# A two-block transformer on one core: differential attention moved beside its own input projection, and single read-outs at the ends of stages

## What is computed

```python
def diff_attention(h, w_in, lq1, lk1, lq2, lk2, subln_w, w_out, rel_table, lambda_init):
    qkv = h @ w_in
    q, k, v = jnp.split(qkv, 3, axis=-1)
    q = q.reshape(B, S, DA_HEADS, 2, DA_HEAD_DIM)
    k = k.reshape(B, S, DA_HEADS, 2, DA_HEAD_DIM)
    v = v.reshape(B, S, DA_HEADS, DA_V_DIM)
...
        logits = jnp.einsum('bqhmd,bkhmd->bmhqk', qb, kb).astype(jnp.float32) * scale + bias
        logits = jnp.where(dist >= 0, logits, -jnp.inf)
        p = jax.nn.softmax(logits, axis=-1)
        attn = p[:, 0] - lam * p[:, 1]
        outs.append(jnp.einsum('bhqk,bkhd->bqhd', attn.astype(vb.dtype), vb))
...
    o = rmsnorm(o, subln_w) * (1.0 - lambda_init)
    return o.reshape(B, S, DA_HEADS * DA_V_DIM) @ w_out
```

## Time and profile before

| | us |
|---|---|
| median of 3 runs | 1363.32 (1362.34 to 1363.82) |
| the profiled execution, its own time | 1364.6 |
| its span | 1362.9 |
| PE busy in the span | 1303.9 (96%) |
| DVE busy | 926.0 (68%) |
| ACT busy | 730.5 (54%) |

### The profile page before, as it was taken

How to read it: one execution, slowest core, us unless ns; L and a number is a source line. 1 busy time by engine, 2 the same in 40 slices (tenths; PEclk the granted TensorE clock), 3 DMA queues, 4 the chain that set the end, 5 groups by cost and what they waited for, 6 DMA issues and landing times.

```text
span 1362.9 us, 24156 instructions
## 1 busy us (share of the span) xinstructions
PE 1303.9 (96%) x8322; PEld 1153.5 (85%) x8322; DVE 926.0 (68%) x1573; ACT 730.5 (54%) x1300; POOL 265.6 (19%) x274
## 2 busy tenths in 40 slices
PE   7998999999999999999999979999999987999997
PEld 5986668999999988888889957888889975888885
DVE  6766755655555798776556688886657766877564
ACT  5456644666444455664444475665445755566441
POOL 3001101222010113441010002442104610344010
PEclk9996557999999999999999989999999998999997
DMA  7331021565554655655565503665464531665540
GB/s 233 112 119 54 0 63 47 178 182 182 184 185 155 214 173 169 185 186 190 191 205 174 173 28 96 204 193 186 161 209 126 186 124 31 185 185 185 186 154 31
DMA packets 204435, 205.28 MB, mean 151 GB/s; under 512 B 6079, under 2 KB 203829, under 8 KB 204361
## 3 DMA queue, kind: packets, MB, share of 16 engines
q1 hardware_dynamic: 202101, 202.73, 47.2%
q10 hardware_dynamic: 2260, 1.58, 0.4%
HBM read 203.22 MB, written 1.06 MB: 150 GB/s over the span
## 4 chain that ended last, share of the span: by engine, by line
PE 81%; DVE 11%; ACT 4%; issue 1%; POOL 1%; DMA 0%; DVEq 0%; SPq 0%; POOLq 0%; ACTq 0%
PE PS L1437 27%; PE PS L1438 14%; PE PS L1432 9%; PE PS L1431 9%; PE PS L1433 9%; DVE wlo L859 3%; PE PS L1613 3%; PE PS L1592 3%; DVE x L836 2%; DVE tmp L872 1%; PE PS L1635 1%; PE PS L1601 1%; ACT whi L444 1%; DVE h L882 1%; PE PS L1549 1%
## 5 line engine op out<-in xcount | busy, mean ns | idle before, releaser
L859 DVE TENSOR_TENSOR wlo<-raw,whi 128x1024 fp32r<-128x1024 f32 (+1 forms) x388 | 469.1, 1211 | 210.2 <-ACT whi L444 208.4
L444 ACT ACTIVATE whi<-raw 128x1024 fp32r<-128x1024 f32 (+1 forms) x388 | 404.1, 1045 | 361.6 <-PE PS L1438 212.1
L1437 PE MATMUL PS<-x,whi 128*128 128x512 f32 x832 | 293.8, 397 | 4.9 <-DVE x L836 4.5
L1431 PE MATMUL PS<-x,whi 128*128 128x256 f32 (+2 forms) x928 | 265.7, 286 | 7.6 <-DVE wlo L859 4.2
L1437 PE MATMUL PS<-hid,whi 128*128 128x512 f32 x768 | 267.0, 394 | 0.0
L1432 PE MATMUL PS<-x,whi 128*128 128x256 f32 (+2 forms) x928 | 265.3, 286 | 0.0
L1433 PE MATMUL PS<-x,wlo 128*128 128x256 f32 (+2 forms) x928 | 263.8, 284 | 0.0
L1438 PE MATMUL PS<-x,wlo 128*128 128x256 f32 x832 | 235.1, 283 | 0.0
L1438 PE MATMUL PS<-hid,wlo 128*128 128x256 f32 x768 | 212.7, 277 | 0.0
L1437 PEld LDWEIGHTS PS<-x,whi 128*128 128x128 f32 x832 | 157.1, 189 | 42.9 <-DVE x L836 6.8
L1343 POOL TENSOR_TENSOR acc<-acc,sq 128x256 f32<-128x256 f32 (+2 forms) x72 | 64.9, 901 | 652.7 <-ACT sq L472 651.9
(11 more groups left out here) (274 smaller groups left out, 1710.3 us busy)
## 6 DMA issues: line engine op xcount, KB each, us to landing
raw<-in_mlp_w SPq DMA_DIRECT2D x64, 1024.0 KB, 5.7
raw<-in_w_mlp_up SPq DMA_DIRECT2D x32, 1024.0 KB, 5.5
raw<-in_w_mlp_down SPq DMA_DIRECT2D x32, 1024.0 KB, 5.2
raw<-in_w_in_conv SPq DMA_DIRECT2D x12, 1024.0 KB, 5.1
raw<-in_attn_w_in SPq DMA_DIRECT2D x12, 1024.0 KB, 5.2
raw<-in_mlstm_w_in SPq DMA_DIRECT2D x12, 1024.0 KB, 5.3
raw<-in_w_in_attn SPq DMA_DIRECT2D x9, 1024.0 KB, 8.0
raw<-in_w_out_attn SPq DMA_DIRECT2D x4, 1024.0 KB, 8.5
```

What stands on the lines that cost most here:

```text
L444: A(part_view(whi, b), raw_view(b), ACT.Copy).then_inc(w_hi, 1)
L859: V.tensor_tensor(part_view(wlo, b), raw_view(b), f32(part_view(whi, b)), ALU.subtract).then_inc(w_lo, 1)
L1431: mm(dst, whi_b, xs_hi, start=first, stop=False)
L1437: mm(dst.rearrange("p (a t) -> p a t", a=2), std_cols(whi[b % RING], k), xs_both, start=first, stop=False)
```

## The change

**Attention beside d_in.** The blocks of d_in come in the order q, k, v of one pair of heads (two blocks each), then the next pair. One loop over 62 **slots** drives PE, ACT and DVE. In slots 0 to 47 PE does half a block of d_in (4 of 8 k); in slots 48 to 53 it does k 0 to 2 and then 3 to 5 of the first three blocks of d_out, in slot 57 their k = 6, and after the last slot their k = 7 and the blocks 3 to 7. The four tiles of pair p have slots 12p+10, 13, 16, 19; the last pair's have 46, 48, 50, 52. For a tile in slot s: scores and max in s, exp in s+1, probabilities in s+2, transposes and their copy in s+4, the product with V in s+5; a head's norm and y follow 5 to 8 slots behind its second tile. The values are transposed head by head into the small bank MISC. Banks: 3 for d_in's results instead of 4, one for each map, one for transposes, one for the head's output.

**Scores.** Plain fp32, one matmul for each map over 128 or 256 columns, straight from `dz`; `dzh` and `dzl` and their splitting are gone.

**Single read-out.** The last block of c_in, c_out, d_out and m_out and the block o = 3 of each half of dn1, dn2 and dn3 run as products, and DVE reads them without `halves`.

The diff, cut to its core:

```diff
-    dz = sb("dz", [P, KB * S], F32, s)
-    dzh, dzl = sb("dzh", [P, 2 * KB * S], F32R, s), sb("dzl", [P, 2 * KB * S], F32R, s)
+    dz = sb("dz", [P, 3 * KB * S], F32, s)
...
+    if stage == "d_in":
+        return D_IN_BANK[o % 3]
     return (O[stage] + o) % PSR
...
-MAP_BANK = ((0, 1), (2, 5))
+MAP_BANK = (5, 6)
 A_SPLIT_AT = tuple(NT * HEADS + 3 * n for n in range(RING))
-D_FLIP_AT = (4, 7)
-D_T_BANK = 3
+D_FLIP_AT = (5, 8)
+D_TILE_AT = {12 * p + 10 + (2 if p == 3 else 3) * r: 4 * p + r for p in range(4) for r in range(4)}
+D_VALUE_AT = {12 * p + 11 + 2 * e: 2 * p + e for p in range(4) for e in range(2)}
+D_SLOTS = 62
+D_T_BANK, D_O_BANK, D_IN_BANK = 2, 7, (3, 0, 1)
...
-            residual(n, j, tok, (psum_read, O[stage] + j + 1) if n == 1 else (Z["out_h"], KB * (n // 2 - 1) + j + 1))
+            residual(n, j, tok, (psum_read, O[stage] + j + 1) if n == 1 or j == KB - 1 else (Z["out_h"], (KB - 1) * (n // 2 - 1) + j + 1))
...
-            act.wait_ge(Z["cs_ready"], f + 1)
+            if f < KB - 1:
+                act.wait_ge(Z["cs_ready"], f + 1)
+            else:
+                act.wait_ge(psum_read, O["c_in"] + j + 1)
             A(at(yh, f, LAST), cs[:, f % 2, :], ACT.Copy).then_inc(Z["y_hi"], 1)
...
+    for s in range(D_SLOTS):
+        n = d_tile(s - 1)
+        if n is not None:
             d_exp(n)
...
+        hd = D_VALUE_AT.get(s)
+        if hd is not None:
+            act.wait_ge(Z["d_vt"], hd + 1)
+            A(dvt[:, :, hd * P:(hd + 1) * P], PS[:, MISC, 0:S].rearrange("p (a c) -> p a c", a=TS), ACT.Copy)\
+                .then_inc(Z["d_vtok"], 1)
+        n = d_tile(s - 4)
+        if n is not None:
+            d_prob_t(n)
...
-            A(d_sq[:, hd % 2, :], PS[:, O_BANK[hd % 2], 0:S], ACT.Square).then_inc(Z["d_osq"], 1)
-        hd = head_at(n, 6)
...
+        hd = d_head(s - 7)
...
+        if s < 6 * KB and s % 2:
+            split_hi(B["d_in"] + s // 2 + RING)
...
-            if n == 1:
+            if n == 1 or j == KB - 1:
                 V.tensor_tensor(at(h, j, tok), PS[:, bank(stage, j), 0:tok[1]], at(h, j, tok), ALU.add).then_inc(psum_read, 1)
             else:
                 halves(tmp[:, j % 2, 0:S], bank(stage, j)).then_inc(psum_read, 1)
...
-                    if m:
...
                     else:
                         mul(t, PS[:, bank(dn, o), 0:tok[1]], rstd2[:, 0:tok[1]]).then_inc(psum_read, 1)
...
+            if f < KB - 1:
+                halves(tmp[:, f % 2, 0:S], bk).then_inc(psum_read, 1)
+                dve.wait_ge(psum_read, O["c_in"] + j + 1)
+                mul(cs[:, f % 2, :], tmp[:, f % 2, 0:S], cy[:, f, :]).then_inc(Z["cs_ready"], 1)
+            else:
+                mul(cs[:, f % 2, :], PS[:, bk, 0:S], cy[:, f, :]).then_inc(psum_read, 1)
...
     norm(4, LAST)
-    dve.wait_ge(w_used, B["d_in"])
-    for j in range(3 * KB):
-        dve.wait_ge(w_used, B["d_in"] + j + 1)
-        dst = d_z(j) if j < 2 * KB else zb(dz, j - 2 * KB)
-        if 4 <= j < 2 * KB:
-            dve.wait_ge(Z["d_lo"], j - 3)
-        mul(dst, PS[:, bank("d_in", j), 0:S], rstd[:, 0:S]).then_inc(psum_read, 1)
-        split_lo(B["d_in"] + j + RING)
-        if 2 <= j < 2 * KB + 2:
-            dve.wait_ge(Z["d_hi"], j - 1)
-            V.tensor_tensor(zb(dzl, j - 2), d_z(j - 2), f32(zb(dzh, j - 2)), ALU.subtract).then_inc(Z["d_lo"], 1)
...
+    for s in range(D_SLOTS):
+        if s < 6 * KB and s % 2:
+            j = s // 2
+            dve.wait_ge(w_used, B["d_in"] + j + 1)
+            mul(d_z(j), PS[:, bank("d_in", j), 0:S], rstd[:, 0:S]).then_inc(psum_read, 1)
+        n = d_tile(s)
+        if n is not None:
+            if n == 0:
+                dve.wait_ge(Z["d_bias"], 2)
             d_max(n)
-        if n >= 7 and (n - 7) % TS == 0 and (n - 7) // TS < HEADS:
...
+        n = d_tile(s - 2)
+        if n is not None:
+            d_prob(n)
+        hd = d_head(s - 7)
...
-        if 2 <= n < N_D + 2:
-            d_prob(n - 2)
-        if n >= 9 and (n - 9) % TS == 0 and (n - 9) // TS < HEADS:
...
+        hd = d_head(s - 8)
+        if hd is not None:
...
+        if s < 6 * KB and s % 2:
+            split_lo(B["d_in"] + s // 2 + RING)
     out_proj("d_out", 5, LAST)
...
-        if O[stage] + o >= PSR:
-            pe.wait_ge(psum_read, i + (O[stage] + o - PSR + 1))
-    def linear(stage, j, xhi, xlo, tok, ready=None, i=0, o=None, pair=False):
+        banks = 3 if stage == "d_in" or stage == "d_out" and o < 3 else PSR
+        if O[stage] + o >= banks:
+            pe.wait_ge(psum_read, i + (O[stage] + o - banks + 1))
...
+        if ks[0] == 0:
+            free_bank(stage, o, i)
+            pe.wait_ge(w_lo, i + (b + 1))
         order = [k for k, _ in ready[1]] if ready else range(KB)
         for n, k in enumerate(order):
+            if n not in ks:
+                continue
...
+        if ks[-1] == KB - 1:
+            last.then_inc(w_used, 1)
...
-            linear(stage, j, yh, yl, tok, (Z["y_ready"], ready) if j == 0 else None, pair=mixer > 0)
+            linear(stage, j, yh, yl, tok, (Z["y_ready"], ready) if j == 0 else None, pair=mixer > 0 and j < KB - 1)
...
-                    if m:
+                    if m and o != 3:
                         last = paired(b, k, hid(hh, kk, S), both_hid(kk, S), PS[:, bank(dn, o), :], kk == 0, kk == FB - 1)
                     else:
                         last = product(b, k, std_cols, hid(hh, kk, tok[1]), hid(hl, kk, tok[1]),
...
+        linear("c_in", j, xh, xl, HALOED if j < 2 * KB else LAST, x_blocks(2) if j == 0 else None, pair=2 * KB <= j < 3 * KB - 1)
...
+    def d_values(hd):
+        pe.wait_ge(psum_read, O["d_in"] + 6 * (hd // 2) + 4 + hd % 2 + 1)
+        d_section()
         for a in range(TS):
...
+            c = (2 * KB + hd) * S + a * P
+            last = nc.tensor.transpose(PS[:, MISC, a * P:(a + 1) * P], dz[:, c:c + P], ident[:, :])
         last.then_inc(Z["d_vt"], 1)
...
+    def d_scores(n):
+        hd, i = n // TS, n % TS
+        w = P * (i + 1)
+        if n == 0:
             pe.wait_ge(Z["d_bias"], 2)
...
-    def d_scores(n):
-        hd, i = n // TS, n % TS
-        if n >= 2:
-            pe.wait_ge(Z["d_max"], n - 1)
+        if n >= 1:
+            pe.wait_ge(Z["d_max"], n)
+        pe.wait_ge(psum_read, O["d_in"] + 6 * (hd // 2) + 4)
         for m in range(2):
             rows = slice(DV * m, DV * m + DV)
-            dst = PS[:, MAP_BANK[m][n % 2], 0:S]
...
-            mm(dst, dzh[rows, q], dzh[rows, k], start=True, stop=False)
-            mm(dst, dzh[rows, q], dzl[rows, k], start=False, stop=False)
-            last = mm(dst, dzl[rows, q], dzh[rows, k], start=False, stop=True)
+            q, k = slice(hd * S + i * P, hd * S + (i + 1) * P), slice((KB + hd) * S, (KB + hd) * S + w)
+            last = mm(PS[:, MAP_BANK[m], 0:w], dz[rows, q], dz[rows, k], start=True, stop=True)
         last.then_inc(Z["d_s"], 1)
...
+            if hd >= 1:
+                pe.wait_ge(Z["d_res"], hd)
...
-    pe.wait_ge(psum_read, O["d_out"])
-    pe.wait_ge(Z["d_lo"], 2 * KB)
-    d_scores(0)
-    pe.wait_ge(Z["d_vtok"], 1)
-    d_values(1)
-    for n in range(N_D + 4):
-        if n + 1 < N_D:
-            d_scores(n + 1)
-        if 3 <= n < N_D + 3:
-            d_output(n - 3)
...
+    def d_squares(hd):
+        pe.wait_ge(Z["d_osq"], hd + 1)
+        d_section()
+        mm(PS[:, MISC, 0:S], ones[:, :], d_sq[:, hd % 2, :], start=True, stop=True).then_inc(Z["d_ss"], 1)
+        section[0] = (Z["d_ln"], hd + 1)
...
+    def d_out_part(j, ks):
+        linear("d_out", j, yh, yl, LAST, (Z["y_ready"], [(k, 16 + k + 1) for k in range(KB)]), pair=True, ks=ks)
...
+    for s in range(D_SLOTS):
+        if s < 6 * KB:
+            linear("d_in", s // 2, xh, xl, LAST, x_blocks(4) if s < 2 else None,
+                   ks=range(s % 2 * (KB // 2), (s % 2 + 1) * (KB // 2)))
+        elif s < 6 * KB + 6:
+            third = (s - 6 * KB) // 3
+            d_out_part(s % 3, range(3 * third, 3 * third + 3))
+        elif s == 6 * KB + 9:
+            for j in range(3):
+                d_out_part(j, range(6, 7))
+        if s == 3:
+            norm(4, S)
+        if s in D_FLIP_AT:
+            d_flips(D_FLIP_AT.index(s))
+        n = d_tile(s)
+        if n is not None:
+            d_scores(n)
+        hd = D_VALUE_AT.get(s)
+        if hd is not None:
+            d_values(hd)
+        n = d_tile(s - 4)
+        if n is not None:
+            d_transpose(n)
+        n = d_tile(s - 5)
+        if n is not None:
+            d_output(n)
+        hd = d_head(s - 6)
+        if hd is not None:
+            d_squares(hd)
+    for j in range(3):
+        d_out_part(j, range(7, 8))
+    for j in range(3, KB):
+        linear("d_out", j, yh, yl, LAST, pair=j < KB - 1)
     mlp(2, LAST)
```

118 lines of the change are left out of this document (40 added, 78 removed).

## The result

The changed kernel takes **1371.83 us** (1370.52 to 1372.15, five runs) against 1363.82 of the kernel before measured beside it: ratio 1.0053, 95% interval 1.0038 to 1.0067. It is slower by 0.5%, where 1358.6 was forecast. The profiled execution took 1372.11 us.

The account below looks back on a forecast made before the run. PE, busy 96% of the span, was taken to bound the kernel, with idle time in the attention and at stage ends. Attention -2.7, other ends -4.0, products +2.0: 1363.3 - 4.7 = 1358.6 us; own range 1355 to 1361, with rivals 1353 to 1366.

Parts of the forecast that it names:

- the wait in d_in's slots: Attention work between d_in's blocks: only bank MISC makes PE wait, in slots 25 and 37, 1.3 us in all.
- the tail: From slot 46 to k = 7 of d_out's block 0: 26.6 us, could be 24 to 30.
- up2's start: Behind d_out's end: PE waits longer there, and no time was charged for a lower clock.
- the price of a product: Single read-outs in dn stages and c_in: a product costs 0.010 us more per k than a pair, +2.0 in all.
- The slower rival: Slots in d_in not covered, a late `wlo` on DVE stalls PE: +12, 1370, or milder +6, 1364.6; chance 0.17.
- The wait for head 5's y: In the tail, ahead of k = 5 of d_out's block 0: PE idles 2.5 us.
- the second rival: The granted clock falls in the new tail, PE's work on the chain takes twice as long: +3, 1361.6; chance 0.16.
- The blocks after it are covered by DVE's backlog: d_out's blocks behind the tail: a low clock in the tail costs nothing there.
- Early pieces of d_out worth nothing: d_out's first three blocks, begun early, gain nothing beyond the tail, since DVE reads blocks 3.09 us apart.
- The gain of the read-outs: Chain 0.72 us shorter at each of six ends (c_out, dn1, d_out, dn2, m_out, dn3), 0.36 at c_in's.
- Plain fp32 scores worth nothing: A head's scores take 1.1 to 1.3 us either way; the splits taken away are hidden beside d_in.

Follow-up runs that it names:

- e8_split2: The changed kernel with ACT's `split_hi` moved behind the copy of the probabilities, ahead of square and norm: 1368.22 us, ratio 1.0016 to before.
- e7_early0: The changed kernel with only block 0 of d_out begun early, blocks 1 and 2 run whole behind its k = 7: 1370.01 us, ratio 1.0030 to before.
- e9_filltail: e7_early0 plus 28 matmuls of no use (128 columns) in PE's waits behind slot 48: 1364.25 us, ratio 0.9988 to before.
- e6_fill: The changed kernel plus 12 matmuls of no use ahead of k = 5, 6, 7 of up2's first block: 1372.63 us, ratio 1.0046 to before.
- e15_a31: e10_best plus filling in the first mixer's attention, 3 matmuls per tile for the first 22 tiles, then 1: median 1325.96 us, ratio 0.9704 to before.
- e10_best: e9_filltail plus ACT's new order, pairs in dn stages, stages begun with blocks side by side, filled last-mixer waits: 1349.22 us, ratio 0.9891 to before.

## Why the prediction was wrong

The steps that failed are the wait in d_in's slots, put at 1.3; the tail, put at 26.6 at full clock; up2's start, where the clock was put at nothing; and the price of a product, 0.010. They are 4.3, 3.7, 1.9 and 3.0 of the miss.

- *Waits in d_in's slots, "I charge only the bank MISC", 1.3.* Failed, +4.3. The loads of the engines were right (they had two slots to spare), but I counted work per head and not the order inside ACT's slot, where `split_hi` stood behind a wait for PE. The edit was a move, and I did not walk through what stood in front of each moved instruction. The 1.3 for the bank MISC came (1.1 in two waits); the 3.8 for `d_o` was at nothing. e8_split2 gives the time back.
- *The slower rival, a `wlo` late at some place in DVE's queue, +6 (chance 0.17).* The mechanism that came, with another cause (ACT's order, not DVE's load) and about two thirds of the milder size.
- *The tail, 22.8 behind d_out's first piece.* It took 26.5, +3.7. The wait for head 5's y was placed and sized rightly (2.5 forecast, 2.13 measured). 0.8 was there before it: the bank MISC, charged in slots 25 and 37 but not in the tail, made PE wait 1.30. The other 2.9 came in two stretches at half clock, and are the second rival, +3, chance 0.16. That split is read from the changed kernel's trace; no run fills the waits of this kernel. The rivals were treated as alternatives; they came together, and beside the product's price.
- *"The blocks after it are covered by DVE's backlog."* It held for d_out itself in the changed kernel, 23.8 from k = 7 to k = 7 with two stretches at half clock inside. It is no rule: where the low clock lasted longer, the blocks cost 2.7 (e7_early0 against e9_filltail). And the backlog left PE idle at d_out's end, which brought the clock down in up2 as well: +1.9, gone in e6_fill.
- *Early pieces of d_out worth nothing.* Right: DVE's reads at 3.08 set its end, 23.8 from k = 7 to k = 7 as forecast. By the idle time at the end they were worth less than nothing.
- *The gain of the read-outs, 0.72 per end.* Right at c_out (24.55 to 23.83), at dn1's end and at d_out's.
- *Their cost, 0.010 per k.* Too low: 0.0133 for the product itself, and nothing was charged for the pairs behind it. 1.64 per dn stage against 0.64, 3.0 in all. Of the 1.0 missed in each stage, 0.2 is the product's price, taken from the row of another stage, and 0.8 the slower pairs; the forecast's own range had no term for either.
- *Plain fp32 scores worth nothing.* Not tried by itself. No wait of PE in d_in is for its scores.

Forecast -4.7, plus 9.9 and 3.0, is +8.2, beside +7.5 in the profiles and +8.0 in the medians. That it closes this well is partly luck: the first attention, up0, up1 and the last mixer, which the sum leaves out, moved by -1.8, +0.8, -1.5 and +1.1.

## To carry to other kernels

When independent work is woven into a stage, walk down each in-order queue, and ask of every instruction that others need (a weight split, a load) what it now stands behind; one line in the wrong place cost more than the whole move gained. A loop that is busy 100% at a granted clock of 0.50 need not be PE-bound by its work (the first attention took 23 us less in e15_a31 than in e10_best, at full clock and with more matmuls in it): look at the clock by stretch before believing a busy share. Where PE's links are on the chain, fill its waits, best with real work from the next blocks, else with matmuls that nothing reads; in the one loop tried where DVE and ACT have most of the work, holding the clock by filling gained nothing.

## What was not expected of the hardware

- Added PE work shortened a kernel: 28 matmuls of 128 columns made 1370.0 into 1364.3, and the filling of the first attention, on top of e10_best, 1349 into 1326 to 1328, but for one run of e15_a31 at 1368.
- The clock does not always fall behind a wait of the same length: 1.25 us brought 20 us of low clock in one execution and none in the profiled executions of two kernels that share it.
- At full clock, fp32r products of 256 columns start 0.120 us apart in the dn stages (0.360 per k), pairs 0.3465 per k, and pairs in a dn stage 0.353 once a product has run in it, even 20 us behind the last one.
